# A two-layer mixer: context and sequence given separate norms, and four weight blocks taken out of seven-product form

## What is computed

```python
def mixer_layer(x, ctx, ...):                     # layer 0 and layer 1
    hx = rms_norm_2(x, g_pre) * (1.0 + scale_x) + shift_x
    hc = rms_norm_2(ctx, g_pre) * (1.0 + scale_c) + shift_c
    (qa_x, ka_x, va_x, za_x, qlb_x, kvlb_x, krb_x, zb_x,
     bc_x, cc_x, uc_x, zc_x, ga_x, gb_x, gc_x) = in_proj(hx, w_in)
    ...                                           # the same of hc; attentions a and b
    yc_x = short_gated_conv(bc_x, cc_x, uc_x, conv_w)
    out_x = merge_branches(ya_x, yb_x, yc_x, za_x, zb_x, zc_x, ga_x, gb_x, gc_x, w_branch, w_o)
    x = x + gate_x * rms_norm_2(out_x, g_post)
    if update_ctx:                                # layer 0 alone
        ...
        ctx = ctx + gate_c * rms_norm_2(out_c, g_post)
```

## Time and profile before

| | |
|---|---|
| time, median of 3 runs | 2528.81 us (2527.99 to 2529.82) |
| profiled execution: its time, its span | 2530.3 us, 2528.5 us |
| TensorE busy | 2402.4 us, 95% |
| VectorE busy | 1566.5 us, 62% |
| ScalarE busy | 1035.0 us, 41% |
| GpSimd busy | 531.5 us, 21% |

### The profile page before, as it was taken

How to read it: one execution, slowest core, us unless ns; L and a number is a source line. 1 busy time by engine, 2 the same in 40 slices (tenths; PEclk the granted TensorE clock), 3 DMA queues, 4 the chain that set the end, 5 groups by cost and what they waited for, 6 DMA issues and landing times.

```text
span 2528.5 us, 37854 instructions
## 1 busy us (share of the span) xinstructions
PE 2402.4 (95%) x14987; PEld 2018.4 (80%) x14987; DVE 1566.5 (62%) x2624; ACT 1035.0 (41%) x1964; POOL 531.5 (21%) x369
## 2 busy tenths in 40 slices
PE   7987889899999999999999999999989999999998
PEld 6764667777788887769987899998866688889998
DVE  4745545453343444587558866975556685788984
ACT  3325543342222233554236423334335553654444
POOL 3004222140210221331004221023423210322021
PEclk9997999999999999999999999999999999999999
DMA  5231143245443321001320112124121024013232
GB/s 172 84 102 34 51 133 118 68 150 167 157 127 100 100 73 42 22 5 42 84 67 1 36 58 84 59 74 138 36 77 34 26 67 117 10 43 113 80 115 95
DMA packets 196657, 199.79 MB, mean 79 GB/s; under 512 B 15832, under 2 KB 189624, under 8 KB 196354
## 3 DMA queue, kind: packets, MB, share of 16 engines
q1 hardware_dynamic: 191106, 178.23, 23.0%
q10 hardware_dynamic: 5376, 19.14, 2.0%
HBM read 186.87 MB, written 10.49 MB: 78 GB/s over the span
## 4 chain that ended last, share of the span: by engine, by line
PE 78%; DVE 11%; ACT 4%; issue 3%; POOL 2%; DMA 1%; SPq 0%; ACTq 0%; DVEq 0%; POOLq 0%
PE PS L917 9%; PE PS L920 9%; PE PS L918 9%; PE PS L871 5%; PE PS L873 5%; PE PS L872 5%; PE PS L1039 4%; PE PS L1069 4%; PE PS L1053 3%; PE PS L844 3%; PE PS L847 3%; PE PS L845 3%; DVE WL L2262 1%; DVE WL L2287 1%; ACT WH L1554 1%
## 5 line engine op out<-in xcount | busy, mean ns | idle before, releaser
L2262 DVE TENSOR_TENSOR WL<-WB,WH 128x2048 fp32r<-128x2048 f32 (+3 forms) x86 | 183.0, 2128 | 243.9 <-ACT WH L1554 234.2
L917 PE MATMUL PS<-HH,WH 128*128 128x512 f32 (+1 forms) x848 | 322.9, 381 | 5.2 <-DVE WL L2262 2.5
L918 PE MATMUL PS<-HL,WH 128*128 128x512 f32 (+1 forms) x848 | 306.5, 370 | 0.0
L920 PE MATMUL PS<-HH,WL 128*128 128x512 f32 (+1 forms) x848 | 287.0, 371 | 0.0
L3290 POOL TENSOR_SCALAR SA<-SA,ST 128x768 f32<-128x768 f32 (+4 forms) x80 | 143.7, 1796 | 522.4 <-DVE ST L2430 522.4
L1554 ACT ACTIVATE WH<-WB 128x2048 fp32r<-128x2048 f32 (+3 forms) x86 | 148.1, 1722 | 157.8 <-PE PS L920 93.7
L871 PE MATMUL PS<-SH,WH 128*128 128x384 f32 (+1 forms) x640 | 199.1, 311 | 3.6 <-DVE WB L2321 3.5
L2287 DVE TENSOR_TENSOR WL<-WB,WH 128x512 fp32r<-128x512 f32 x240 | 182.1, 773 | 30.1 <-ACT WH L1570 30.1
L1570 ACT ACTIVATE WH<-WB 128x512 fp32r<-128x512 f32 x240 | 141.8, 624 | 142.2 <-DVE WB L2274 123.8
L917 PEld LDWEIGHTS PS<-HH,WH 128*128 128x128 f32 (+1 forms) x848 | 156.6, 185 | 52.2 <-issue 11.0
L873 PE MATMUL PS<-SH,WL 128*128 128x384 f32 (+1 forms) x640 | 198.0, 309 | 0.0
(11 more groups left out here) (425 smaller groups left out, 5872.9 us busy)
## 6 DMA issues: line engine op xcount, KB each, us to landing
WB<-in_w_in_dram SPq DMA_DIRECT2D x61, 1024.0 KB, 5.3
WB<-in_w_ff_dram SPq DMA_DIRECT2D x32, 1024.0 KB, 5.5
WB<-in_w_mod_dram SPq DMA_DIRECT2D x24, 1024.0 KB, 5.2
WB<-in_w_branch_dram SPq DMA_DIRECT2D x24, 512.0 KB, 3.5
WB<-in_w_o_dram SPq DMA_DIRECT2D x8, 1024.0 KB, 5.8
WB<-in_w_in_dram SPq DMA_DIRECT2D x14, 512.0 KB, 6.3
WB<-in_cmp_w_dram SPq DMA_DIRECT2D x4, 1024.0 KB, 5.6
WB<-in_w_mkv_dram SPq DMA_DIRECT2D x4, 1024.0 KB, 5.2
```

The costliest lines, as they stand in the source:

```text
L917: pe.matmul(D[0:m, d + o:d + o + w], h, xh[:, o:o + w], start=first, stop=False)
L918: pe.matmul(D[0:m, d + o:d + o + w], h, xl[:, o:o + w], start=False, stop=False)
L920: t = pe.matmul(D[0:m, d + o:d + o + w], lo, xh[:, o:o + w], start=False, stop=last)
L2262: dve.tensor_tensor(b.of(WL[i]), b.of(WB[b.n % NW]), b.of(WH[i]).bitcast(F32), ALU.subtract).then_inc(*done("wl", s))
```

## The change

Four things move. (1) The context's norm `h0c` is made within the group e2 of the feed-forward net (`context_norm`); after e3 TensorE goes straight to the query tiles' context columns (`queries_of_context`), with the sums and the spreading of the sequence between them, then their sequence columns. (2) Tiles 4 to 7 of `o0` are made on the sequence alone, and their context columns afterwards, between the sums and spreads of the sequence (`output_of_context`, `sums_between`, `spread_between`); norm and halves of layer 1 are made for the sequence first and for the context later, under `ql1` tile 2 and `kvl1` (`queries_beside`, `latents_beside`). (3) The fillers (`warm`) at both places are gone. (4) `bc1` and `z21` are plain blocks. Nothing changes in the order of SyncE's loads. The splits of `ql1` and `kvl1` stand at other places in the orders of ScalarE and VectorE.

```diff
@@ weight_blocks
-            cut(f"z{b}{l}", W[:, zc:zc + 512], ring="sums" if b == 2 else "plain")
+            cut(f"z{b}{l}", W[:, zc:zc + 512], ring="sums" if b == 2 and l == 0 else "plain")
...
-        cut(f"bc{l}", W[:, 2464:2976], ring="sums")
+        cut(f"bc{l}", W[:, 2464:2976], ring="plain" if l else "sums")
...
+        if l == 0:
+            for b in out[-2:]:
+                b.freed = ("lin", "o0c", 2 * b.part + 1)
@@ tensor_program
+                    if (g, h) == (2, 0):
+                        ps.pin(("norm", "h0c"), 4)
+                        pe.wait_ge(*at("nadd", "h0c", 7))
+                        add_columns(PS[4], 0, NC, RB[rb["h0c"]], True, True).then_inc(*done("nsum", "h0c"))
+                    if (g, h) == (2, 1):
+                        spread_columns("h0c", NC)
...
+            def queries_beside():
+                b = of["ql1"][0]
+                D = slot(("ql1", 0), ("qll", 1, 0), ("qll", 1, 1))
+                wh, wl = whole(b)
+                for k in range(8):
+                    pe.wait_ge(*at(*low1("x", k)))
...
+                sums_between("c")
+                for k, _ in enumerate(linear("ql1", hx(NX), NX, lambda j: [("qll", 1, j)], parts=[1], pace=1)):
+                    if k == 3:
+                        spread_between("o0", "c")
+                    if k == 6:
+                        spread_between("h1", "c")
+            def queries_of_context():
...
+                Ds = [slot(("ql0", j), ("qll", 0, j)) for j in range(2)]
+                whole(of["ql0"][0])
+                for k in range(8):
+                    if k == 4:
+                        sum_columns_late("h0x", 8, NX, ("hn", "h0x", 7))
+                    pe.wait_ge(*at(*low1("c", k, 0)))
+                    for j in range(2):
+                        part(j, Ds[j], k, "c")
+                spread_columns("h0x", NX)
+                Ds.append(slot(("ql0", 2), ("qll", 0, 2)))
+                whole(of["ql0"][1])
+                for k in range(8):
+                    part(2, Ds[2], k, "c")
+                for js in ((0, 1), (2,)):
+                    for k in range(8):
+                        pe.wait_ge(*at(*low1("x", k, 0)))
+                        for j in js:
+                            part(j, Ds[j], k, "x")
+            def latents_beside():
+                wh, wl = whole(of["kvl1"][0])
+                for o, n, e in ((0, NX, "x"), (NX, NC, "c")):
+                    for j in range(2):
...
+                            if e == "c" and j == 0:
+                                pe.wait_ge(*at(*low1("c", k)))
...
-                drain(linear(f"o{l}", hx(nt), nt, lambda j: [("ot_a", l, j)], parts=[1, 2, 3]))
...
-                spread_columns(N, nt)
-                spread_columns("h1", nt, 4)
+                drain(linear("o0", hx(NT), NT, lambda j: [("ot_a", 0, j)], parts=[1]))
+                drain(linear("o0", hx(NX), NX, lambda j: [("ot_a", 0, j)], parts=[2, 3]))
...
+                output_of_context(4)
+                sums_between("x")
+                spread_between("o0", "x")
+                output_of_context(5)
+                spread_between("h1", "x")
+                output_of_context(6)
+                output_of_context(7)
@@ scalar_program
+                kept("c", 4)
+                root_between("o0", "x")
+                root_between("h1", "x")
+                kept("c", 5)
+                begin("o0", 3)
+                high1("x", 0)
+                high1("x", 1)
...
+                for f in range(8 if l else 0):
+                    high1("c", f)
+                    if f == 0:
+                        begin("ql1", 1)
@@ vector_program
+                for f in range(8):
+                    normed("x", f)
+                    if f == 1:
+                        begin("o0", 3)
+                    if f:
+                        low_half1("x", f - 1)
+                    if f < 3:
+                        with_root("x", f + 5)
+                    if f == 3:
+                        cross("c", 5)
+                    if f == 5:
+                        cross("c", 6)
+                low_half1("x", 7)
+                begin("ql1")
...
+                    for f in range(8):
+                        if f < 3:
+                            with_root("c", f + 5)
+                        normed("c", f)
+                        if f:
+                            low_half1("c", f - 1)
+                        if f == 1:
+                            begin("ql1", 1)
```

More of the change, by code:

```diff
@@ L1387, in tensor_program @@
[L1387 to L1388 removed]
+                if l == 0:
+                    queries_of_context()
+                else:
+                    queries_beside()
+                    ps.order = four
                 def query_sums(j):
@@ L1964, in scalar_program @@
                         step += 1
-            act.wait_ge(*at("modm"))
+                    if (g, j) == (2, 1):
+                        root("h0c", NC, 1024)
+                    if g == 2 and j > 3:
+                        for f in (2 * j - 8, 2 * j - 7):
+                            act.wait_ge(*at("hn", "h0c", f))
+                            act.activation(HH[:, f, NX:NT], SD[sd["hn", "h0c", f]][:, NX:NT], ACT.Identity, bias=MOD[:, 0, f, 1:2]
+                                           ).then_inc(*done("hh", "h0c", f))
@@ new lines, in root_between @@
+            def root_between(N, e):
+                o, n, _ = sides1[e]
+                m, c, w = "" if e == "x" else "c", o // 128, n // 128
+                D = RS[:, rs[N], :] if m else taken(rs, [RS[:, i, :] for i in range(4)], N, ("nbc", N + "c"))
+                act.wait_ge(*at(*(("nsum", "o0" + m) if N == "o0" else ("uv", e, 3))))
+                src = P("norm", "o0")[:, o:o + w] if N == "o0" else D[:, c:c + w]
+                act.activation(D[:, c:c + w], src, ACT.Sqrt, bias=EP[:, 0:1], scale=1.0 / 1024).then_inc(*done("nroot", N + m))
@@ L2861, in vector_program @@
                         mod_next()
-            dve.wait_ge(*at("modb", 23))
-            for l in range(2):
-                for i, (name, base, one, op) in enumerate((("g_pre", 8, 1.0, ALU.add), ("g_post", 16, 0.5, ALU.mult))):
-                    r = rows[name] + 8 * l
-                    g = VC[:, r // 128, r % 128:r % 128 + 8].unsqueeze(2).to_broadcast([128, 8, 2])
-                    t = dve.scalar_tensor_tensor(GM[:, l, i, :, :], MOD[:, l, base:base + 8, :], one, g, op, ALU.mult)
-            t.then_inc(*done("modm"))
@@ L2869, in vector_program, with cross @@
-            dve.wait_ge(*at("modm"))
+                    if g == 2:
+                        context_norm(j)
+            def cross(e, f):
+                full = e == "x" and f < 4
+                o, n, _ = (0, NT, 0) if full else sides1[e]
+                tail = ("c",) if e == "c" else ()
+                D = AC[0] if f == 0 else taken(("cross", *tail, f), ("nsum", "h1" + "".join(tail)) if f == 7 else ("cross", *tail, f, "sum"))
+                dve.wait_ge(*at(*out_kept(e, f)))
+                dve.tensor_tensor(D[:, o:o + n], XTc[:, f, o:o + n], OT[:, f, o:o + n], ALU.mult).then_inc(*done("cross", *tail, f))
+                if 0 < f < 7:
+                    dve.wait_ge(*at("cross", *tail, f))
+                    dve.tensor_tensor(AC[0][:, o:o + n], AC[0][:, o:o + n], D[:, o:o + n], ALU.add).then_inc(*done("cross", *tail, f, "sum"))
@@ L2910, in vector_program @@
-                begin(f"ql{l}")
-                low_parts(7)
+                    begin("ql0")
+                    dve.wait_ge(*at("nroot", "h0x"))
+                    dve.tensor_copy(HS[:, 0:4], P("norm", "h0x")[:, 0:4]).then_inc(*done("hsum", "h0x"))
+                    inverse("h0x", 4)
+                    dve.wait_ge(*at("nbc", "h0x"))
+                    for f in range(8):
+                        normed("x", f, 0)
+                        if f:
+                            low_half1("x", f - 1, 0)
@@ L3033, in outputs @@
                     def outputs():
-                        if b == 2:
+                        if b == 2 and not in_sums(z):
+                            bc_out(2)
+                            yield
+                            conv(3)
+                            yield
+                            bc_out(3)
+                            yield
+                            for j in range(4):
+                                zy(j)
+                                yield
+                                if j < 3:
+                                    yield
+                        elif b == 2:
                             bc_out(2)
@@ L3080, in outputs @@
                         for u in range(4):
-                            for _ in range(7 if u else 4 if b == 2 else 6):
+                            for _ in range(7 if u else 5 if b == 2 and not in_sums(z) else 4 if b == 2 else 6):
                                 yield
@@ L3174, in outputs @@
                         yield
-                        yield
```

(7 more changed lines are left out.)

420 lines of the change are left out of this document (277 added, 143 removed).

## The result

| | before | after |
|---|---|---|
| time, median of 6 runs | 2528.40 us (2525.47 to 2531.77) | 2512.02 us (2509.56 to 2513.98) |
| profiled execution: its time, its span | 2530.3 us, 2528.5 us | 2509.56 us, 2507.8 us |

The account below looks back on a forecast made before the run. TensorE was taken as busy for 95% of the span, with VectorE the bound in `bc1` and `z21`. Gains 8.5 + 8 + 3.8 = 20.3 us off 2530.3 gave 2510.0, less 1.5 for the median 2508.5 us; range 2501 to 2519.

Parts of the forecast that it names:

- e2: Group of the feed-forward net ahead of layer 0: the context's sums and spread add 4 instructions each there, 0.9 us.
- The start of layer 0: From e3's end to `kvl0`, with sums and spread added in e2: 29.7 us against 38.2, gain 8.5 us.
- The weight wait: Ahead of `kvl0`: TensorE waits 1.0 us for its weight halves, as tile 2 covers less of their split.
- the same matmuls remain: Start of layer 0: the same 24 k-steps of 1.04 us stay, 25.0 us.
- some 7 us: Context's norm in e2: without the cover there, its 21 VectorE instructions of 0.35 us would cost this much.
- Between the layers: From `o0` to `kvl1`'s end and the query sum: end at 1870.7 against 1878.8, gain 8 us, bounds 0 and 15.
- the gap ahead of `kvl1`: TensorE waits 4.5 us for `kvl1`'s weight half, split behind the context's first high half, then runs half-clocked, 1.7 us.
- the last low half at T + 23.5: Between the layers: the last low half comes 23.5 us after T = 1812.9, when VectorE may start the norms.
- The idle gaps within the pair: In `ql1`'s pair between the layers: TensorE idles in gaps of 3 to 4 us.
- The slower rival: At `kvl1`: the context side becomes the bound, TensorE waits some 28 us more, 2536 us; chance 0.02.
- Plain quarters: `bc1` and `z21` in layer 1: four plain blocks take 43.9 us against 47.7, gain 3.8 us.
- 5.5, if `g21` starts without arrears: Upper bound on the gain from plain `bc1` and `z21`: 5.5 us if `g21` behind them starts without arrears.

Follow-up runs that it names:

- fillers: The changed kernel with 34 filler matmuls put on TensorE into the gap ahead of `kvl1`: 2521.02 us, ratio 0.9971.
- `kvl1`'s split: The changed kernel with `kvl1`'s weights split earlier, ahead of the context's root on ScalarE and behind its second inverse on VectorE: 2506.58 us, ratio 0.9918.
- after again: The changed kernel without any edit, profiled a second time: span 2513.9 us.
- the pair's buffers: The changed kernel with `o0`'s pair in PSUM buffers 0 and 1, the norm buffers taken behind context tile 4: 2505.69 us, ratio 0.9911.
- all three edits: The changed kernel with `o0`'s pair in buffers 0 and 1, `kvl1`'s weights split earlier, and `kvl0`'s split ahead of the first query tile's eviction: 2498.84 us, ratio 0.9881.
- last version: On top of all three edits, the context root's eight products ahead of its norms, and layer 0's first query tiles in buffers 0 and 1: 2499.26 us, ratio 0.9881.
- sums again: The changed kernel with `bc1` and `z21` again by way of sums: 2518.86 us, ratio 0.9966.
- plain in both layers: The changed kernel with `bc0` and `z20` plain as well: 2519.32 us, ratio 0.9970.
- the norm behind e3: The changed kernel with layer 0's context norm behind the last tile of e3 and not inside e2: 2520.71 us, ratio 0.9970.

## Why the prediction came out as it did

**The total** was right to 3.5 us (2508.5 against 2512.0), inside the range. By the medians, the change took 16.4 us off where 20.3 were forecast. That the profiled executions lie 20.7 us apart, 0.4 from the forecast, is luck twice over: three PSUM buffer effects that no term had, +3.7, +2.6 and -7.4, nearly cancel, and the execution of after met, with two others, the mildest clock between the layers of all that were profiled.

**The start of layer 0**: mechanism right, size 1.7 us too large (6.8 measured, 8.5 forecast). Context matmuls follow e3, the granted clock is 1.00 throughout, no low half is waited for. The weight wait was 1.3 us where 1.0 was said; the edit that moves `kvl0`'s split confirms it. The step that failed is "the same matmuls remain" as the whole of the opening: the first context tile takes a buffer that VectorE frees 0.83 us late. The matmuls themselves were busy for 28.2 us, where the sum has 27.8. The 0.9 us in e2 measured 0.9. The bound on an uncovered norm, "some 7 us", was 5.0 by stage.

**Between the layers**: the forecast path holds step by step. From `o0`'s end to the norm's spread 14.4 us (14.9 forecast); the pair's end 22.7 us later (25); context sums, tile 2 and two spreads 9.1 us (9.1); the gap ahead of `kvl1` 4.6 us (4.5); `kvl1` with its clock loss and the query sum 19.9 us (19.2). So the term mis-sized is "the last low half at T + 23.5": it ended at 1830.3, 20.4 us behind the spread (1809.9), so that VectorE and POOL were 3.1 us faster. In the second execution of the same kernel the stretch is 2.8 us longer, so the stage's gain is 7.4 to 10.2 us, and 8 lies within it. The idle gaps within the pair were 0.7 to 1.75 us, four in number, and not "3 to 4 us". The clock dip at the column sums came (0.82 and 0.83 from 1800 to 1810). The gap ahead of `kvl1` was put down to the weight half alone; the queue was the right one, but TensorE stood there for the norm's PSUM buffer as well, as the fillers show. The slower rival is excluded.

**Plain quarters**: mechanism right, 5.0 us against 3.8. The bound "5.5, if `g21` starts without arrears" was the right case, and the stall of the earlier trace rows, which `g21` has too (1.48 us at 2404.42 and 0.91 at 2415.51 before), should have made it the value: 1.2 us of the gain are in `g21`'s first block (16.65 us from 2405.89 before, 15.42 after).

**What was left out**: The prediction followed every instruction of a moved step through engines and queues, and not through PSUM. The order of instructions does not show which buffer a tile takes. The diff does, in lines such as `ps.order = [2, 3, 0, 1]`, and the cost could have been worked out from the rows of before: b2's last result is taken by VectorE behind a weight split of 3.8 us and two low halves of 5.1, and the pair of before did not wait for it.

**VectorE beside POOL.** The same instruction, a product of 256 columns, took 1.50 us while POOL worked on an addition and 0.42 us where POOL was idle; of after, VectorE, POOL, VectorE:

```profile
1819.20 1.50 DVE L3081 TENSOR_TENSOR SD<-XTc,OT 128x256 f32<-128x256 f32 x1
1817.34 3.07 POOL L3659 TENSOR_TENSOR XTc<-XTc,OT 128x512 f32<-128x512 f32 x2
1831.38 0.42 DVE L3081 TENSOR_TENSOR SD<-XTc,OT 128x256 f32<-128x256 f32 x1
```

POOL's second addition ends at 1820.4 and the product at 1820.7, 0.3 us behind it: it stood still for the rest of POOL's instruction and then ran alone. The split of a weight block likewise took 3.82 us at 1728.66 beside a busy POOL and 2.27 us at 1839.08 with POOL idle. The page SBUF — State Buffer of the Trainium skill (Who interferes with whom) says that VectorE and GpSimd, where they contend, exclude each other for a whole instruction; these rows agree. The prediction made its test of this the time of the last low half, some 3 us sooner if bandwidth were shared. It came 3.1 us sooner, which says little either way, since the 23.5 us held 5 to 6 us that were taken over from the old stretch with its other order of instructions.

**The clock behind a wait.** The waits of 7.2 and 4.6 us cost 1.75 and 2.1 us of clock behind them (the second 1.3 us in two other executions, last section), the wait of 2.03 us in the kernel before 1.8 us; the waits of 0.83 and 1.29 us at the front cost none. The Trainium skill (TensorE: Matmul & The Clock Gate, What's actually happening) says that the throttled state is the default and activity releases it, by which a removed filler is a loss wherever a wait is left. For the longer waits the trace agrees that a wait has this price; whether a filler within one of them would have saved it, no run here shows.

## What to carry to other kernels

When a piece of work moves, write down for every tile behind it which buffer it takes and what frees that buffer, PSUM's too: one list of four numbers was worth about 4 us in a kernel that was otherwise as before, and 6 us the other way ahead of `o0`. A weight split belongs in the queue as soon as its home is free, ahead of a chain that waits for TensorE, as at `kvl0` and `kvl1` here; ahead of a result that has to leave PSUM it delays whoever takes that buffer, as at `o0`. Fewer multiplications pay only while the engine that prepares them keeps up: the same exchange of sums for plain products won 5 us where VectorE was at its limit and lost 7 where it was not (there with tiles of 768 columns).

## What was not expected of the hardware

The clock fell between the layers while TensorE was busy without a pause, in one-column sums and short spreads with context matmuls before and behind; of after, with TensorE busy for all 5 us of each:

```profile
1800.00:1805.00 5.00, 5.00 (x39) 5.00 (x39) 1.40 (x6) 0.56 (x2) 0.39 (x1) 0.82 0.01 3
1805.00:1810.00 5.00, 5.00 (x38) 5.00 (x38) 3.24 (x7) 0.90 (x3) 3.51 (x3) 0.83 0.00 2
```

And in the same order of instructions it fell by different amounts. Two pieces show it best: the sums, the spread and context tile 5 (80 instructions in all kernels), and the last three k-steps of `ql1`'s pair behind its wait of 1.8 us. Each is given from its first matmul's start to its last one's end:

| profiled execution | sums, spread, tile 5 | last three k-steps |
|---|---|---|
| after; `kvl1`'s split; fillers | 10.8 us each | 4.5 us |
| after again; the pair's buffers | 12.4 us each | 6.0 us |
| all three edits | 12.5 us | 4.5 us |
| last version | 12.4 us | 6.0 us |
| sums again; plain in both layers | 14.0 us each | 4.5 us |
| the norm behind e3 | 14.0 us | 6.0 us |

The values lie on three steps 1.6 us apart, and on two steps 1.4 us apart. In "sums again" and "plain in both layers" the second dip came one piece later: from the context's sums to the first spread, three k-steps of `ql1`'s tile 2 took 3.6 and not 2.2 us, with TensorE busy all along. In these two the wait of 4.6 us also cost less behind it, 18.1 us for `kvl1` and not 19.0. From `o0`'s first matmul to `kvl1`'s end, with what `o0`'s own tiles lose, it is 126.8 us in the execution of after, 129.7 in its second one, 131.1 and 131.4 in those two and 132.3 with the norm behind e3, at the same waits. One record group of the sums, 8 records, in the execution of after and in that of the norm behind e3:

```profile
1802.52 1.19 PE L1006 MATMUL PS<-CM,SA 128*128 128x1 f32 x8
```

```profile
1809.05 1.84 PE L1006 MATMUL PS<-CM,SA 128*128 128x1 f32 x8
```

Windows over the last three k-steps, in the kernel with three edits and in the last version, which are alike there:

```profile
1819.00:1824.00 5.00, 5.00 (x29) 4.06 (x27) 3.22 (x5) 1.60 (x2) 0.00 (x0) 1.00 0.44 125
```

```profile
1822.00:1828.00 6.00, 6.00 (x23) 4.80 (x22) 3.47 (x5) 0.95 (x3) 0.00 (x0) 0.72 0.47 148
```

The granted clock is 1.00 in one and 0.72 in the other. What decides it in one execution was not found. It makes up to 5.5 us of the spread between executions, as much as some edits here are worth, and it is why an edit of 1 us was read from its stage and not from the medians.
